# Down-projection weights of an expert loaded as two 64-partition transfers with two neighbouring rows per partition

## The chip, the cores and the metric

The kernel runs on one core of a Trainium2 chip. The metric is the device time of one execution in microseconds. Three runs of the kernel before gave 993.53, 995.6 and 988.67 us (median 993.53).

## The reference, cut to what matters

One step of a one-layer encoder over 320 tokens (256 of a prompt, 64 of a sample) of width 1024. Its first part (projections, mLSTM, spatial gating, memory attention, output projection) isn't touched. Its second part is a mixture of 32 experts of inner width 256, of which each token takes two out of one group of eight:

```
for e in range(N_EXPERTS):                                  # 32
    hidden = jax.nn.silu(xf @ w_g[e]) * (xf @ w_u[e])       # w_g, w_u: 1024 x 256
    y = y + combine[:, e:e + 1] * (hidden @ w_d[e])         # w_d: 256 x 1024
```

Each expert has three matrices of 1 MB in float32, so the mixture reads 96 MB of weights.

## The kernel before, in words

The program is written by hand, engine by engine, with semaphores. After the first part (until about 660 us of the span) comes `level`, the mixture. Up to 128 tokens of each of the four groups are gathered once, and then the 32 experts are taken in order, x = 0 to 31.

**Units of weights.** The list `STREAM` cuts the weights into 96 units of 1 MB: for each expert "A" (the first half of the rows of gate and up), "B" (the second half) and "D" (down). The order is A0 B0 A1 B1 D0 A2 B2 D1 and so on. There are six slots (`NS`), and unit u goes to slot u % 6. A slot holds the raw float32 unit (`raw_w`, 2048 numbers on each of 128 partitions), and beside it the same unit split into a high part and a rest (`w_r`), since a product is made of three products of such parts.

**Path of a unit.** SP (`load_unit`, L478) waits until PE has used the unit six places before (`m_used`), then issues two transfers of 512 KB, with 16 DMA engines below them (L498 for D, L503 for A and B). ACT waits for both (`m_full`) and copies the raw unit to its high part (`unit_high`, L889). DVE subtracts to get the rest (`unit_rest`, L1183). Then PE uses it: `gate_up` (L776) for A and B, `down` (L798) for D. The slot is free only when PE is done.

**Order on PE.** `gate_up` x part A, `hidden_T` of x - 1, `gate_up` x part B, `down` of x - 1, and on most experts a small `scatter` (L812) of the group before. `gate_up` is 12 matmuls of 512 columns for each part, `down` is 12. `hidden_T` (L786) transposes the hidden values of the expert (128 slots x 256, on DVE written to `hid` by L1481) with two transposes of 128 x 128 each, so that `hidT[:, .., c, :]` has on partition d the hidden index that the weights of `w_r[.., c*D : (c+1)*D]` have on partition d.

**Layout of D before.** The transfer k (0 or 1) puts rows k*128 to k*128+127 of the 256 x 1024 matrix on the 128 partitions, one row of 4 KB each. So partition d holds rows d and 128 + d, and transpose c takes the columns c*128 to c*128+127 of `hid`.

A and B have runs of 4 KB too: four rows of 256 numbers, on all 128 partitions.

Of the kernel before, what the change touches and what calls it, by code (L numbers as in the profile page):

```python
# [23 lines left out]
D = 1024  # L24
# [19 lines left out]
NS = 6  # L44
# [157 lines left out]
def build_kernel(nc, ins, outs):  # L202
    I, O = ins, outs
    ctx = ExitStack()
    with ctx:
# [109 lines left out]
        hid = at(SP0 + 3 * UW + G * 384, 2, DE)  # L315
# [26 lines left out]
        ident = sb("ident", [128, 128])  # L342
# [42 lines left out]
        ms = ctx.enter_context(nc.psum_tensor("ms", [128, 4, 512], FP32))  # L385
# [37 lines left out]
        m_full = [sem(f"expert_unit_full{i}") for i in range(NS)]  # L423
# [33 lines left out]
        @block.sync  # L457
        def _(sp):
            for i, (t0, n) in enumerate(TILES):
                src = I["x_prompt"][0, t0:t0 + n, :] if i < 2 else I["x_sample"][0, :, :]  # L460
                sp.dma_start(x_tm[0:n, i, :], src).then_inc(s_x, 16)
            for i in range(2):
                sp.dma_start(mem_tm[:, i, :], I["mem_prompt"][0, i * 128:(i + 1) * 128, :]).then_inc(s_mem, 16)
            for r0, name in ((P_MIX, "norm_mix_g"), (P_MEM, "mem_norm_g"), (P_MOE, "norm_moe_g"), (P_HN, "mlstm_norm_g")):
                sp.dma_start(prows[r0:r0 + 8, :], I[name][0, :].rearrange("(c p) -> c p", p=128)).then_inc(s_par2, 16)
            sp.dma_start(prows[P_CW:P_CW + 64, :], I["mlstm_conv_w"][0].rearrange("j (c p) -> (j c) p", p=128)).then_inc(s_par2, 16)
            sp.dma_start(prows[P_CB:P_CB + 16, :], I["mlstm_conv_b"][0, :].rearrange("(c p) -> c p", p=128)).then_inc(s_par2, 16)
            sp.dma_start(srows[0:48, :], I["state_mlstm_conv"][0, 0].rearrange("j (c p) -> (j c) p", p=128)).then_inc(s_par2, 16)
            sp.dma_start(srows[48:56, :], I["state_mlstm_n"][0, 0].rearrange("h (c p) -> (h c) p", p=128)).then_inc(s_par2, 16)
            for n, (name, col) in enumerate(UNITS):  # L470
                if n >= RING:
                    for e in "DP":
                        sp.wait_ge(u_lo[e], n - RING + 1)
                src = I[name][0, :, col:col + 256].rearrange("(k p) n -> p k n", p=128)
                sp.dma_start(ringw[:, n % RING, :].rearrange("p (k n) -> p k n", n=256), src).then_inc(unit_full[n % RING], 16)


            def load_unit(lv, u):  # L478
                x, part = STREAM[u]
                if isinstance(lv, int) and u < NS:  # L480
                    if u == 0:
                        sp.wait_ge(*done("gate", 1, 7))
                    elif u == 1:
                        sp.wait_ge(*done("br", 0, 7))
                    elif u == 2:
                        sp.wait_ge(*done("br", 1, 7))
                        sp.wait_ge(s_gvout, 16)
                    elif u == 4:
                        for e in "DP":
                            sp.wait_ge(u_lo[e], len(UNITS))  # L490
                else:
                    sp.wait_ge(m_used, NU * lv + u - NS + 1)
                if u == NS - 1:
                    sp.wait_ge(m_gather, NQ * (lv + 1))
                dst = raw_w[u % NS]
                if part == "D":
                    for k in range(2):
                        sp.dma_start(dst[:, k * D:(k + 1) * D], I["w_exp_down"][0, x, k * 128:(k + 1) * 128, :]).then_inc(m_full[u % NS], 16)  # L498
                else:
                    k0 = 0 if part == "A" else 4  # L500
                    for j, name in enumerate(("w_exp_gate", "w_exp_up")):
                        src = I[name][0, x].rearrange("(p k) n -> p k n", k=KC)[:, k0:k0 + 4, :]
                        sp.dma_start(dst[:, j * D:(j + 1) * D].rearrange("p (k n) -> p k n", n=DE), src).then_inc(m_full[u % NS], 16)  # L503

            for u in range(NU):
                load_unit(0, u)
            sp.wait_ge(*done("ranks"))
            need = sp.value_load(more[0:1, 0:1], min_val=0, max_val=LEVELS - 1)
            with sp.Fori(1, LEVELS) as lv:
                with sp.If(need >= lv):  # L510
                    for u in range(NU):
                        load_unit(lv, u)
            for i, (t0, n) in enumerate(TILES):
                sp.wait_ge(s_fin, i + 1)
                dst = O["y_prompt"][0, t0:t0 + n, :] if i < 2 else O["y_sample"][0]
                sp.dma_start(dst, y_tm[0:n, i, :]).then_inc(s_yout, 16)
            sp.wait_ge(s_yout, 48)
# [3 lines left out]
        def _(pe):  # L521
            mm, tr = nc.tensor.matmul, nc.tensor.transpose
# [12 lines left out]
            for s in STEPS:  # L535
# [7 lines left out]
                if s["ring"] == "pj":  # L543
                    n = s["unit"]
# [3 lines left out]
                if kind in ("mq", "qk", "o", "u", "gate", "br"):  # L548
                    c = a[-1]
                    src = xn_r  # L550
                    if kind == "mq":
                        pe.wait_ge(s_xnl, 3)
                    if kind == "br":
                        src = u_r if a[0] == 1 else br_r
# [6 lines left out]
                    last = project_parts(s, 128, T, lambda k, p, q: (w[:, p, k, (c % 2) * 128:(c % 2) * 128 + 128], src[:, q, k, :]))  # L561
                elif kind in ("memk", "memv"):
                    if kind == "memk":
                        pe.wait_ge(s_mnl, 2)
                    last = project_parts(s, 128, 256, lambda k, p, q: (mn_r[:, p, k, a[1] * 128:a[1] * 128 + 128], w[:, q, k, :]))
                elif kind in ("v", "gv"):
                    t0, n = TILES[a[1]]
                    last = project_parts(s, n, 256, lambda k, p, q: (xn_r[:, p, k, t0:t0 + n], w[:, q, k, :]))
                elif kind == "res":
                    t0, n = TILES[a[1]]  # L570
                    pe.wait_ge(s_mixl, 8)
                    last = project_parts(s, n, 256, lambda k, p, q: (mix_r[:, p, k, t0:t0 + n], w[:, q, k, :]))
                elif kind == "xT":
                    i, half = a
                    n = TILES[i][1]
                    pe.wait_ge(s_xs, i + 1)
                    for j in range(4):
                        last = tr(b[:, j * 128:j * 128 + n], xs_tm[0:n, i, (4 * half + j) * 128:(4 * half + j + 1) * 128], ident[0:n, 0:n])
                elif kind == "memT":
                    i, half = a  # L580
                    pe.wait_ge(s_xs, 4 + i)
                    for j in range(4):
                        last = tr(b[:, j * 128:j * 128 + 128], mem_tm[:, i, (4 * half + j) * 128:(4 * half + j + 1) * 128], ident[:, :])
                elif kind == "params":
                    pe.wait_ge(s_const, 2)
                    pe.wait_ge(s_par2, 16 * 8)
                    last = tr(b[:, 0:P_ALL], prows[0:P_ALL, :], ident[0:P_ALL, 0:P_ALL])
                elif kind == "state":
                    last = tr(b[:, 0:56], srows[0:56, :], ident[0:56, 0:56])
                elif kind in ("gi", "gf"):  # L590
# [3 lines left out]
                    last = project(s, H, T, [(wif[:, k, o:o + H], xnT[:, k, :]) for k in range(KC)])  # L594
                elif kind == "cols":
                    pe.wait_ge(s_g4, 1)
                    for i, (t0, n) in enumerate(TILES):
                        for q, r in enumerate((R_A, R_IG, R_F)):
                            c0 = (i * 3 + q) * H
                            last = tr(b[0:n, c0:c0 + H], rows[0:H, r, t0:t0 + n], ident[0:H, 0:H])  # L600
                elif kind == "bc":
                    last = mm(b[:, 0:T + TS + 1], sel[0:H, a[0], :], rb[0:H, :], start=True, stop=True)
                elif kind == "wsT":
                    pe.wait_ge(s_ws, 16)
                    for g in range(H):
                        last = tr(b[:, g * 128:g * 128 + 128], ws[:, g, :], ident[:, :])
                elif kind == "ka":
# [5 lines left out]
                    for dk in range(2):  # L613
                        for j in range(2):
                            src = memk[:, j, h * HD + dk * 128:h * HD + dk * 128 + 128] if which == 0 else cmk[:, h % 2, j, dk * 128:dk * 128 + 128]
                            last = tr(b[:, dk * 256 + j * 128:dk * 256 + j * 128 + 128], src, ident[:, :])
                elif kind == "sc":
# [3 lines left out]
                    for q, i in enumerate((0, 1) if which == 0 else (2,)):  # L621
                        t0, n = TILES[i]
                        for dk in range(2):
                            last = mm(b[0:n, q * 256:q * 256 + 256], mqT[:, 2 * h + dk, t0:t0 + n], kmT[:, h % 2, which, dk, :], start=dk == 0, stop=dk == 1)
                elif kind == "pt":
                    h, which = a
                    pe.wait_ge(s_prob, 2 * h + which + 1)
                    for j in range(2):
                        for i in ((0, 1) if which == 0 else (2,)):
                            n = TILES[i][1]  # L630
                            c0 = j * 256 + i * 128 if which == 0 else j * 64
                            last = tr(b[:, c0:c0 + n], probs[0:n, h % 2, i, j * 128:j * 128 + 128], ident[0:n, 0:n])
                elif kind == "av":
# [5 lines left out]
                    t0, n = (0, TP) if which == 0 else (TP, TS)  # L639
                    for dk in range(2):  # L640
                        for j in range(2):
                            v = memv[:, j, h * HD + dk * 128:h * HD + dk * 128 + 128] if which == 0 else cmv[:, h % 2, j, dk * 128:dk * 128 + 128]
                            last = mm(b[:, dk * n:dk * n + n], v, pT[:, h % 2, j, t0:t0 + n], start=j == 0, stop=j == 1)
                elif kind == "cvT":
                    pe.wait_ge(s_tail, 32)
                    last = tr(b[0:48, 0:128], cvo[:, a[0], :], ident[:, :])
                elif kind == "kt":
                    h, which = a
                    pe.wait_ge(s_silu, 8 + 2 * h + 2)
                    for i in ((0, 1) if which == 0 else (2,)):  # L650
                        t0, n = TILES[i]
                        for dk in range(2):
                            c0 = (i % 2) * 256 + dk * 128
                            last = tr(b[0:n, c0:c0 + 128], qkT[:, 8 + 2 * h + dk, t0:t0 + n], ident[:, :])
# [5 lines left out]
                elif kind == "num":  # L660
# [5 lines left out]
                    if i == 0:  # L666
                        last = mm(b[:, 0:w1], st[:, 0:128], v_tm[:, 0, h, 0:w1], start=True, stop=True)
# [112 lines left out]
            def hidden_T(lv, x):  # L780
                pe.wait_ge(m_hid, E * lv + x + 1)
                until(pe, m_htl, E * lv + x - 1)
                if x < 2:
                    pe.wait_ge(m_combined, lv + 1)
                for c in range(2):
                    last = tr(ms[:, x % 2, c * 128:c * 128 + 128], hid[:, x % 2, c * 128:c * 128 + 128], ident[:, :])  # L786
                last.then_inc(m_ht, 1)

            def down(lv, x):
# [895 lines left out]
```

## Time and profile before

| | us |
|---|---|
| median of three runs | 993.53 |
| the profiled execution | 991.24 |
| its span | 989.5 |
| PE busy in the span | 898.8 |
| DVE busy | 594.8 |
| ACT busy | 473.1 |

The span counts from the first instruction to the last, and 1.74 us of the profiled time lie around it. PE is the matmul engine, PEld its weight loads, which run beside it. DMA share is the mean busy share of the 16 DMA engines, GB/s is what they moved, and PEclk is the granted TensorE clock (1.00 is 2.4 GHz, 0.50 is 1.2 GHz).

### The profile page before, as it was taken

What the parts mean: (1) busy time and instruction counts of PE and PEld (TensorE: products, weight loads), DVE (VectorE), ACT (ScalarE), POOL (GpSimd) and SP (SyncE); (2) the same over time, 40 slices, a digit from 0 to 9 for tenths busy, and PEclk for the clock granted to TensorE, in tenths of its full rate; (3) what the DMA queues carried; (4) which work ended last, traced back from release to release, by engine and by line L of the source; (5) the groups of instructions that cost most, each with busy time, mean ns of one, the idle gap of its engine ahead of it and who ended that gap; (6) DMA issues with size and microseconds to landing.
All of it is one profiled execution on the core that took longest, in us unless ns stands there. A gap on an engine that the chain in (4) does not pass through costs nothing.

```text
span 989.5 us, 13338 instructions
## 1 busy us (share of the span) xinstructions
PE 898.8 (91%) x5322; PEld 796.4 (80%) x5322; DVE 594.8 (60%) x794; ACT 473.1 (48%) x571; POOL 250.9 (25%) x161
## 2 busy tenths in 40 slices
PE   1889999888999989888999999869999999999993
PEld 0588998878989889888999999838877887787881
DVE  2734257884133254378354444584888889889874
ACT  4344345442433133334323333357777677767752
POOL 3145543333442444243443444100000000000000
PEclk9999999998999999989999999969999999999996
DMA  8225642333347856943423348204999999999951
GB/s 244 85 91 166 213 154 81 97 97 116 123 148 97 108 157 88 138 139 119 148 88 126 128 128 276 108 0 174 350 353 348 352 347 343 350 348 355 348 201 56
DMA packets 102502, 182.68 MB, mean 185 GB/s; under 512 B 8345, under 2 KB 74593, under 8 KB 102434
## 3 DMA queue, kind: packets, MB, share of 16 engines
q1 hardware_dynamic: 95488, 171.55, 54.2%
q0 software_dynamic: 2640, 7.66, 3.6%
q10 hardware_dynamic: 4306, 2.54, 1.3%
q8 instruction: 45, 0.74, 0.3%
q14 instruction: 23, 0.19, 0.1%
HBM read 175.90 MB, written 5.82 MB: 184 GB/s over the span
## 4 chain that ended last, share of the span: by engine, by line
PE 55%; DMA 10%; DVE 5%; ACT 4%; POOL 2%; issue 2%; DVEq 0%; SPq 0%; ACTq 0%
PE pj L526 25%; PE pj L776 14%; PE pj L798 8%; DMA arena<-in_w_in 8%; POOL unit_r L1586 2%; DMA arena<-in_w_exp_down 2%; ACT unit_r L882 2%; PE ms L812 1%; PE ms L700 1%; PE ms L699 1%; ACT w_r L889 1%; DMA arena<-in_w_exp_up 1%; PE ms L526 1%; PE ms L741 1%; DVE w_r L1183 1%
## 5 line engine op out<-in xcount | busy, mean ns | idle before, releaser
L1586 POOL TENSOR_TENSOR unit_r<-arena,unit_r 128x1024 fp32r<-128x1024 f32 x64 | 210.4, 3289 | 326.9 <-ACT unit_r L882 326.9
L526 PE MATMUL pj<-xn_r,unit_r 128*128 128x320 f32 x1536 | 237.3, 313 | 9.6 <-POOL unit_r L1586 9.0
L1183 DVE TENSOR_TENSOR w_r<-arena,w_r 128x2048 fp32r<-128x2048 f32 x96 | 218.9, 2289 | 44.5 <-ACT w_r L889 44.2
L526 PEld LDWEIGHTS pj<-xn_r,unit_r 128*128 128x128 f32 x1536 | 228.4, 190 | 14.1 <-issue 12.7
L1174 DVE TENSOR_TENSOR unit_r<-arena,unit_r 128x1024 fp32r<-128x1024 f32 x64 | 85.0, 1329 | 233.5 <-ACT unit_r L882 233.5
L889 ACT ACTIVATE w_r<-arena 128x2048 fp32r<-128x2048 f32 x96 | 183.5, 1917 | 46.1 <-DMA arena<-in_w_exp_up 30.7
L776 PE MATMUL pj<-w_r,xg 128*128 128x512 f32 x768 | 190.8, 398 | 0.0
L776 PEld LDWEIGHTS pj<-w_r,xg 128*128 128x128 f32 x768 | 141.9, 189 | 30.5
L882 ACT ACTIVATE unit_r<-arena 128x2048 fp32r<-128x2048 f32 x64 | 121.9, 1905 | 62.2 <-PE pj L526 28.9
L798 PE MATMUL pj<-w_r,hidT 128*128 128x512 f32 x384 | 93.1, 391 | 3.0 <-DVE w_r L1183 1.5
L798 PEld LDWEIGHTS pj<-w_r,hidT 128*128 128x128 f32 x384 | 71.6, 188 | 20.1 <-DVE w_r L1183 3.6
L526 PE MATMUL pj<-unit_r,xn_r 128*128 128x256 f32 (+1 forms) x576 | 71.9, 286 | 6.3 <-POOL unit_r L1586 6.3
L526 PEld LDWEIGHTS pj<-unit_r,xn_r 128*128 128x128 f32 (+1 forms) x576 | 70.0, 177 | 6.8 <-issue 6.7
L526 PE MATMUL pj<-br_r,unit_r 128*128 128x320 f32 x384 | 59.7, 311 | 0.0
L526 PEld LDWEIGHTS pj<-br_r,unit_r 128*128 128x128 f32 x384 | 56.6, 188 | 1.4 <-issue 1.1
L526 PEld LDWEIGHTS pj<-unit_r,mn_r 128*128 128x128 f32 x384 | 48.0, 197 | 5.8 <-issue 4.7
L526 PE MATMUL pj<-unit_r,mn_r 128*128 128x256 f32 x384 | 49.6, 290 | 2.9 <-POOL unit_r L1586 2.9
L526 PE MATMUL pj<-unit_r,mix_r 128*128 128x256 f32 (+1 forms) x288 | 35.8, 288 | 2.2 <-DVE mix_r L1178 2.2
L526 PEld LDWEIGHTS pj<-unit_r,mix_r 128*128 128x128 f32 (+1 forms) x288 | 35.5, 178 | 2.5 <-issue 2.5
L1284 DVE SCALAR_TENSOR_TENSOR arena<-arena,prT 128x323 f32<-128x323 f32 x48 | 34.7, 722 | 1.7
L987 ACT ACTIVATE arena<-pj 128x320 f32<-128x320 f32 x24 | 10.4, 435 | 46.5 <-PE pj L526 46.4
L1074 ACT ACTIVATE hidT<-ms 128x256 fp32r<-128x256 f32 x32 | 12.3, 384 | 37.1 <-PE ms L786 36.7
(303 smaller groups left out, 844.9 us busy)
## 6 DMA issues: line engine op xcount, KB each, us to landing
arena<-in_w_in SPq DMA_DIRECT2D x40, 1024.0 KB, 5.3
arena<-in_w_exp_gate SPq DMA_DIRECT2D x64, 512.0 KB, 4.5
arena<-in_w_exp_up SPq DMA_DIRECT2D x64, 512.0 KB, 6.0
arena<-in_w_exp_down SPq DMA_DIRECT2D x64, 512.0 KB, 5.2
arena<-in_w_mem_k SPq DMA_DIRECT2D x4, 1024.0 KB, 11.3
arena<-in_w_mem_v SPq DMA_DIRECT2D x4, 1024.0 KB, 6.3
arena<-in_w_br_mem SPq DMA_DIRECT2D x4, 1024.0 KB, 7.7
arena<-in_w_br_mlstm SPq DMA_DIRECT2D x4, 1024.0 KB, 5.0
```

The lines of the kernel that those rows point to most:

```text
L526: last = mm(bank_of(s)[0:out_rows, 0:out_cols], l, r, start=k == 0, stop=k == len(pairs) - 1)
L699: mm(b[:, t0:t0 + n], gv_tm[0:n, i, c * 128:c * 128 + 128], wsT[0:n, g, 0:n], start=True, stop=False)
L776: last = mm(pj[:, x % 2, :].rearrange("p (h n) -> p h n", h=2), xg[:, k0 + k, xp, g * SLOTS:(g + 1) * SLOTS], w[:, wp, k, :, :], start=k0 ...
L798: last = mm(pj[:, 2 + half, :], hidT[:, x % 2, xp, c, :], w_r[u % NS][:, wp, c * D + half * 512:c * D + half * 512 + 512], start=e == 0 an ...
L882: af(unit_r[n % RING][:, 0, :], ringw[:, n % RING, :], ACT.Copy).then_inc(u_hi, 1)
L889: af(w_r[u % NS][:, 0, :], raw_w[u % NS], ACT.Copy).then_inc(m_hi, 1)
L987: af(sg[:, k % 2, :], b[:, 0:T], ACT.Sigmoid).then_inc(free, 1)
L1074: af(hidT[:, x % 2, 0, :, :].rearrange("p a b -> p (a b)"), ms[:, x % 2, 0:DE], ACT.Copy).then_inc(m_hth, 1)
L1174: v.tensor_tensor(unit_r[n % RING][:, 1, 0:UW // 2], ringw[:, n % RING, 0:UW // 2], unit_r[n % RING][:, 0, 0:UW // 2], ALU.subtract).then_ ...
L1183: v.tensor_tensor(w_r[u % NS][:, 1, :], raw_w[u % NS], w_r[u % NS][:, 0, :], ALU.subtract).then_inc(m_lo, 1)
L1284: ins = v.scalar_tensor_tensor(o, r[:, j:j + CONVW], w(j), o, ALU.mult, ALU.add)
L1586: g.tensor_tensor(unit_r[n % RING][:, 1, UW // 2:], ringw[:, n % RING, UW // 2:], unit_r[n % RING][:, 0, UW // 2:], ALU.subtract).then_inc ...
```

## The change

Both edits keep the count of instructions and their order on each engine. The two transfers of a D unit now have 64 partitions each: transfer q loads rows q*128 to q*128+127, with rows 2p and 2p+1 of that half side by side on partition q*64 + p, which is one run of 8 KB both in memory and on the partition. A partition d then holds rows 2d and 2d + 1 of the matrix. To match this, transpose c of the hidden values takes the columns 2d + c, every second one.

```
                 if part == "D":
-                    for k in range(2):
-                        sp.dma_start(dst[:, k * D:(k + 1) * D], I["w_exp_down"][0, x, k * 128:(k + 1) * 128, :]).then_inc(m_full[u % NS], 16)
+                    for q in range(2):
+                        src = I["w_exp_down"][0, x, q * 128:(q + 1) * 128, :].rearrange("(p c) n -> p (c n)", c=2)
+                        sp.dma_start(dst[q * 64:(q + 1) * 64, :], src).then_inc(m_full[u % NS], 16)
...
                 for c in range(2):
-                    last = tr(ms[:, x % 2, c * 128:c * 128 + 128], hid[:, x % 2, c * 128:c * 128 + 128], ident[:, :])
+                    last = tr(ms[:, x % 2, c * 128:c * 128 + 128], hid[:, x % 2, :].rearrange("p (d c) -> p c d", c=2)[:, c, :], ident[:, :])
```

All line numbers behind L498 grow by one in the changed kernel. A D unit is still 1 MB in two transfers of 512 KB, and the matmuls, their operands' sizes and the copies of ACT and DVE stay as they were.

## Rows read from the trace of the kernel before

**Rows 1.** The page, part 2: span in 40 slices (24.7 us each)

```profile
PE   1889999888999989888999999869999999999993
...
DMA  8225642333347856943423348204999999999951
GB/s 244 85 91 166 213 154 81 97 97 116 123 148 97 108 157 88 138 139 119 148 88 126 128 128 276 108 0 174 350 353 348 352 347 343 350 348 355 348 201 56
```

**Rows 2.** Busy time by stretch, mixture stage, and the last stretch one expert

```profile
core 0: us, PE busy (x) PEld busy (x) DVE busy (x) ACT busy (x) POOL busy (x), PEclk, DMA share, GB/s
700.00:750.00 50.00, 49.42 (x224) 39.52 (x223) 42.32 (x29) 36.88 (x31) 0.00 (x0) 1.00 0.98 349
850.00:900.00 50.00, 49.65 (x222) 40.27 (x221) 44.46 (x33) 35.05 (x28) 0.00 (x0) 1.00 0.99 349
900.00:950.00 50.00, 49.59 (x222) 40.14 (x221) 45.56 (x35) 35.71 (x32) 0.00 (x0) 1.00 0.98 348
680.00:968.00 288.00, 283.69 (x1260) 228.36 (x1259) 245.23 (x181) 197.88 (x166) 0.00 (x0) 1.00 0.93 330
891.38:900.36 8.98, 8.98 (x42) 7.33 (x41) 8.01 (x7) 5.92 (x4) 0.00 (x0) 1.00 1.00 352
```

**Rows 3.** Who waited for whom, 690 to 980 us: us, times, longest

```profile
DVE w_r L1183 <- ACT w_r L889: 33.2, 51, 1.6
ACT w_r L889 <- DMA arena<-in_w_exp_up: 28.7, 35, 2.2
ACT w_r L889 <- DMA arena<-in_w_exp_down: 15.0, 24, 1.2
```

**Rows 4.** The down transfers, all of them, from issue to landing

```profile
DMA to landing us min/median/max: 3.6/5.2/7.1
```

**Rows 5.** The store of y at the end: issues, then busy time by stretch

```profile
983.73 1.53 SPq L516 DMA_DIRECT2D out_y_prompt<-arena  x2
986.11 0.55 SPq L516 DMA_DIRECT2D out_y_sample<-arena  x1
...
985.00:987.00 2.00, 0.00 (x0) 0.00 (x0) 1.09 (x1) 0.00 (x0) 0.00 (x0) 0.50 1.00 406
987.00:988.00 1.00, 0.00 (x0) 0.00 (x0) 0.00 (x0) 0.00 (x0) 0.00 (x0) 0.50 0.89 217
988.00:989.00 1.00, 0.00 (x0) 0.00 (x0) 0.00 (x0) 0.00 (x0) 0.00 (x0) 0.50 0.45 98
```

**Rows 6.** The loads of x at the start: issues, then busy time by stretch

```profile
1.73 0.58 SPq L461 DMA_DIRECT2D arena<-in_x_sample  x1
2.35 1.06 SPq L463 DMA_DIRECT2D arena<-in_mem_prompt  x2
...
6.00:7.00 1.00, 0.00 (x0) 0.00 (x0) 0.00 (x0) 0.00 (x0) 1.00 (x3) 1.00 1.00 168
7.00:8.00 1.00, 0.00 (x0) 0.00 (x0) 0.00 (x0) 0.00 (x0) 0.50 (x1) 1.00 1.01 225
8.00:9.00 1.00, 0.00 (x0) 0.00 (x0) 0.00 (x0) 0.37 (x1) 0.00 (x0) 1.00 0.97 360
```

**Rows 7.** Instructions by line: the transposes, and two strided reads by ACT and DVE

```profile
L786 PEld LDWEIGHTS ms<-ident,arena x64: 137/140/144, 687.4 to 964.3; 128*128 128x128 f32 x64
L786 PE MATMUL ms<-ident,arena x64: 270/272/330, 687.7 to 964.4; 128*128 128x128 f32 x64
L893 ACT ACTIVATE hn_r<-arena x3: 2046/2057/2076, 643.2 to 647.9; 128x1024 fp32r<-128x1024 f32 x2, 64x1024 fp32r<-64x1024 f32 x1
L889 ACT ACTIVATE w_r<-arena x96: 1902/1919/1927, 615.9 to 958.8; 128x2048 fp32r<-128x2048 f32 x96
```

**Rows 8.** Busy time by stretch where the granted clock fell (columns of rows 2)

```profile
221.00:224.00 3.00, 0.00 (x0) 0.00 (x0) 2.89 (x6) 0.05 (x1) 2.31 (x5) 0.92 0.09 10
224.00:228.00 4.00, 2.38 (x6) 1.96 (x7) 3.82 (x9) 2.36 (x3) 0.61 (x1) 0.50 0.79 255
448.00:452.00 4.00, 1.27 (x10) 1.04 (x9) 3.83 (x7) 3.73 (x4) 3.52 (x2) 1.00 0.00 0
452.00:456.00 4.00, 4.00 (x19) 4.00 (x18) 3.96 (x2) 0.00 (x0) 2.19 (x1) 0.57 0.85 263
650.00:655.00 5.00, 5.00 (x14) 1.71 (x12) 5.00 (x3) 4.83 (x3) 0.00 (x0) 0.64 0.00 0
```

## The prediction

> **What bounds the kernel now.** I read the span in slices first [rows 1]. The change lies in the mixture, and the slices show that stage at once: from slice 29 to 38 both PE and the DMA engines stand at 9 tenths, at about 350 GB/s. Elsewhere the DMA engines are half idle, so the mixture is the one long stage in which a slower or faster transfer can count. Second, the busy time by stretch [rows 2]: in 50 us PE is busy for 49.4 to 49.7, and the DMA share is 0.98 or 0.99. For one expert, 891.38 to 900.36 us, PE is busy for 8.98 of 8.98 us. The DMA engines need for the same expert 3 x 1.049 MB = 3.146 MB / 0.350 MB per us = 8.99 us. So two resources are full at once, and neither has room. Over the whole stage, 680 to 968 us, PE lacks 288.0 - 283.7 = 4.3 us. Third, the waits [rows 3]: ACT waits 35 times for an "up" transfer and 24 times for a "down" transfer, 43.7 us in all, and DVE waits 51 times for ACT. The DMA already ends last at ACT, though the copies of ACT and DVE still hide it from PE. Fourth, issue to landing of the down transfers [rows 4]: 5.2 us in the middle for 512 KB, which at 350 GB/s take 1.5 us. So there is always work queued ahead of a transfer, and a slower transfer pushes back all that follow.
>
> **Part 1: transfers of 64 partitions.** What is new is not the bytes but the half of the partitions that each transfer writes. The trace has two transfers of 64 partitions and 4 KB runs, both in 256 KB, each next to transfers of 128 partitions. The store of y [rows 5]: the two prompt transfers move 406 GB/s at a share of 1.00. The sample transfer, with 64 partitions, follows: 217 GB/s at 0.89 (its first part still with the prompt in it), then 98 GB/s at 0.45, which is 98 / 0.45 = 218 GB/s with the engines busy. That is 0.54 of the full rate: all 16 engines are busy, each at about half speed. It is a store, so it reads SBUF where ours writes. The load of x_sample [rows 6] is a load, as ours: behind it the rate is 168 and 225 GB/s for 2 us at a share of 1.00, and 360 once it is through (the transfers behind it have 128 partitions, and share this stretch).
>
> The two halves of a D unit sit behind each other in the same queue, so I expect each engine to do its part of q = 0 and then of q = 1, and at any time most engines write to the same half. The price of a D unit is then 1.049 MB / 0.218 = 4.81 us in place of 1.049 / 0.350 = 3.00 us: 1.81 us more. I take this value, since it is from the row with the clearest cut between full and half width. The bounds: below, 0 us if loads don't show it or if the engines are so far out of step that they use both halves; even less than 0 if the 8 KB runs help (part 2). Above, from the load [rows 6]: (350 - 168) + (350 - 225) = 307 KB were lost in 2 us, which is 0.88 us at 350 GB/s, on a transfer of 0.262 MB; times four for a D unit, 3.5 us.
>
> The Trainium skill speaks against this change. "SBUF — State Buffer", section "Door 1: The DMA port swizzle", says that partitions 0 to 63 reach only half of the 16 ports, and that such a transfer of 1 MiB ran at 196 GB/s against 328 for all partitions. Its section "Can I just issue two DMAs to hit both halves?" says no: two transfers on the two halves were 6% faster than one. By it a D unit takes 1.049 / 0.208 = 5.04 us, 2.04 more than now, and the sum below would be 991.2 + 31 x 2.04 - 7 = 1047 us (an estimate from that page). The store in this trace agrees with it (218 GB/s at full share).
>
> How many D units count: D0 is in the first five units, which land before the stage (share 0.00 in 650 to 655 us, last of [rows 8]). That leaves 31 x 1.81 = 56.1 us of DMA time. What hides some of it: the DMA engines are idle for 1.6% of the 250 us from 700 to 950 us [rows 2], 4 us. And the load starts with a lead of the first units, of which about one unit (3 us) isn't used up now, as PE seldom waits. I take 56 - 4 - 3 = 49 us. Nothing else covers it: PE will wait for a D unit or for the A behind it, about 1.6 us per expert, with ACT and DVE waiting ahead of it. SP's next issue waits for PE in turn, and six slots don't help against a mean rate.
>
> **Part 2: runs of 8 KB.** There are half as many runs. No row shows 8 KB runs in a weight stream. As a bound for the gain, all of D at the clean 406 GB/s of [rows 5] would take 2.58 us, 0.42 less than 3.00: 13 us of DMA time over 31 units. Of these PE could win at most the 4.3 us that it lacks. The other bound is no gain, and I take 0, because the half width sets the rate.
>
> The skill's "DMA: Bandwidth & Descriptors", section "Why small descriptors are slow (HBM only)", gives a fixed cost of some 3 cycles per packet. For 4 KB (128 beats) that is 2.3%, and 8 KB would halve it: an estimate of 0.035 us for a D unit, 1 us in all. No run here shows it.
>
> **Part 3: strided transposes.** Two per expert, 64 in all, now read the hidden values with a step of 8 bytes. PE takes 272 ns for one, its weight load 140 ns [rows 7]. No row shows PE with a strided operand. Below: no change. Above: ACT reads 1024 numbers with a stride in 2057 ns (L893), where 2048 contiguous ones take 1919 ns (L889), so twice per number; twice for PE would be 0.27 us more for each, 64 x 0.27 = 17 us if nothing hid it. I take 0, because where PE waits 1.6 us per expert for the DMA, even the added 0.54 us per expert is covered. Without that cover (the first rival) up to 17 us would show.
>
> **Sum.** 991.2 (the profiled execution) + 49 + 0 + 0 = 1040 us. The profiled execution is 2.3 us under the median of the runs and inside their spread of 988.7 to 995.6, so I leave it so.
>
> **The rivals.**
>
> *A. Half width costs nothing in this stream, and the long runs pay.* For it: the two halves are issued within 1 us of each other, and 16 engines with separate backlogs could drift apart by more than the 1.3 us which a half takes at full rate, so that half the engines write low and half write high partitions. Against it: the drift would have to hold for all engines, as a unit is complete only with the slowest of them, and in [rows 6] the queue was as deep. Time: 991.2 - 4.3 = 987 us at best, 991 without a gain, up to 1008 with the transposes exposed. This is the case that ends on the other side; it decides from the point where a D unit takes under about 3.1 us.
>
> *B. Partly out of step.* The stalls of single engines put some pairs out of step, and half of the 1.81 us stays: 31 x 0.9 - 7 = 21 us, 1012 us.
>
> *C. The damage spreads as in the load at the start.* Engines with 128-partition work wait behind ports that are filled by others. 31 x 3.5 = 108.5, less 7: 102 us, 1093 us. For it is that [rows 6] is a load from the same kind of memory; against it, that other queues and cold buffers share those 2 us.
>
> *D. PE's clock falls in the new waits.* The clock was 0.50 or near it after PE had been busy for 0.00 of 3 us, and again after 1.27 of 4 us [rows 8]. At half clock an expert would need about 18 us of PE. But in my forecast PE is busy for 8.98 of 10.6 us and in one piece stands for under 2 us, so I give this 0.03; it would end above 1080 us.
>
> **How the numbers follow.** The forecast (1020 to 1065 us) has 0.62. B and its neighbours (1004 to 1020) 0.10. C and D (above 1065) 0.14. A has 0.14, of which 0.02 ends over 1% faster and 0.10 within 1%. A measurement of this kernel can tell about 1%, 10 us, from no change, so same is 984 to 1003 us. Slower: 0.62 + 0.10 + 0.14 + the 0.02 of A that is left = 0.88; I shade this to 0.86, same 0.11, faster 0.03. The range runs from 1006, under B, to 1078, between the forecast and C.
>
> **What would show it.** Right: in the changed profile the GB/s of the mixture slices fall from 350 to 290 to 310, with the DMA share still at 0.98 or more; PE falls to 8 tenths; the stretches in which a D unit is moved alone show 200 to 250 GB/s; ACT's wait for "down" grows from 15 us to far over 40; issue to landing of down grows from 5.2 us; L786 stays near 272 ns. Wrong: GB/s still near 350 with PE at 9 tenths (A); a DMA share well under 0.95 with PE waiting would mean that the issue or a wait, not the width, sets the pace; L786 at 400 ns or more would mean part 3 was priced wrongly; a granted clock under 1.00 in the stage is D.

## The result and the profile after

The changed kernel takes 1085.45 us (median of 4 runs, 1080.28 to 1088.63) against 991.43 us for the kernel before (4 runs, 988.67 to 995.6). The ratio is 1.094, with a 95% interval of 1.088 to 1.100: slower, as forecast, but by 94 us in place of 49, and outside my range of 1006 to 1078 us. The profiled execution took 1088.63 us, its span 1086.9 us. One execution of the experiment with sixteen units in a row and one of the looser wait fell in a slower state of the chip, and the ratios leave them out.

The page of the changed kernel, part 2 (40 slices of 27.2 us), which answers to [rows 1]:

```profile
PE   0989999989998997999999977987888877887783
DMA  7244642234558485443334710899999999899871
GB/s 222 78 149 145 212 136 87 89 97 130 131 104 124 99 152 100 154 127 116 117 124 148 271 39 16 248 289 244 244 262 247 267 261 254 243 279 256 222 188 51
```

Outside the mixture the rows have hardly changed. In it the DMA engines are about as busy as before, but move mostly 240 to 290 GB/s in place of 350, and PE falls from 9 tenths to 7 or 8. The stage fills about 13 slices of 27.2 us where it filled 11 of 24.7 us.

The busy time by stretch of the changed kernel (span times, busy time of each engine, granted clock, DMA share, GB/s), which answers to [rows 2] and has its columns:

```profile
700.00:950.00 250.00, 204.05 (x803) 159.09 (x802) 160.40 (x115) 132.08 (x109) 0.00 (x0) 0.92 0.97 256
```

An expert has 3.146 MB, so it now takes 3.146 / 0.256 = 12.3 us. At a share of 0.97 the DMA engines work for 11.9 us of it. Before, it was 9.0 us and 8.8. The stage is about 3 us per expert longer in work alone, where I had expected 1.8.

Who waited for whom in the mixture of the changed kernel (us in all, times, longest), which answers to [rows 3]:

```profile
DVE w_r L1184 <- ACT w_r L890: 129.4, 66, 3.8
PEld ms L787 <- DVE arena L1482: 77.1, 29, 4.1
ACT w_r L890 <- DMA arena<-in_w_exp_up: 75.4, 47, 4.1
ACT w_r L890 <- DMA arena<-in_w_exp_down: 69.0, 30, 3.1
```

Two things are to be seen. PE, which hardly waited, now waits for DVE's hidden values, and DVE in its turn was held by ACT and by the DMA. And ACT waits longer not only for "down", the transfer that was changed (15.0 before, 69.0 now), but just as much for "up", that is for the units A and B (28.7 before, 75.4 now), which were not touched. That was not in my working, and it points to where the missing time is. The page's part 6 says the same of issue to landing (KB each, us in the middle). Before, down took 5.2 us, and gate and up:

```profile
arena<-in_w_exp_gate SPq DMA_DIRECT2D x64, 512.0 KB, 4.5
arena<-in_w_exp_up SPq DMA_DIRECT2D x64, 512.0 KB, 6.0
```

In the changed kernel:

```profile
arena<-in_w_exp_gate SPq DMA_DIRECT2D x64, 512.0 KB, 6.5
arena<-in_w_exp_up SPq DMA_DIRECT2D x64, 512.0 KB, 11.3
arena<-in_w_exp_down SPq DMA_DIRECT2D x64, 512.0 KB, 8.4
```

The two transfers of a unit A or B are issued 0.4 us apart, one behind the other. The middle times of gate and up were 1.5 us apart before and are 4.8 us apart now. This is not the time of up by itself: the two transfers raise the same semaphore `m_full`, by 16 single steps each, and the profile gives the first 16 steps of a unit to gate and the last 16 to up, whichever transfer they came from. What has grown is the time between the first steps of a unit and its last one.

### The profile page after: what moved, and what is told of

Read it like the earlier page. It is cut to its first block, busy times and chain, and to the rows that moved or that the text cites. A ratio compares the mean times of both kernels' runs of the same rounds, so it can differ in the third digit from the quotient of the medians.

```text
span 1086.9 us, 13338 instructions
## 1 busy us (share of the span) xinstructions
PE 934.7 (86%) x5322; PEld 819.1 (75%) x5322; DVE 596.7 (55%) x794; ACT 474.4 (44%) x571; POOL 249.9 (23%) x161
## 4 chain that ended last, share of the span: by engine, by line
PE 39%; DMA 23%; DVE 5%; ACT 5%; issue 4%; POOL 2%; SPq 1%; DVEq 0%; ACTq 0%
PE pj L527 22%; DMA arena<-in_w_exp_down 17%; DMA arena<-in_w_in 7%; PE pj L777 6%; PE pj L799 4%; ACT w_r L890 3%; POOL unit_r L1587 2%; ACT unit_r L883 1%; PE ms L701 1%; PE ms L787 1%; PE ms L700 1%; PE ms L742 1%; DVE arena L1500 1%; SPq L499 1%; PE pj L742 1%
## 5 line engine op out<-in xcount | busy, mean ns | idle before, releaser
L527 PE MATMUL pj<-xn_r,unit_r 128*128 128x320 f32 x1536 | 240.3, 316 | 9.4 <-POOL unit_r L1587 9.2
L527 PEld LDWEIGHTS pj<-xn_r,unit_r 128*128 128x128 f32 x1536 | 231.3, 192 | 14.1 <-issue 12.2
L777 PE MATMUL pj<-w_r,xg 128*128 128x512 f32 x768 | 217.4, 438 | 0.0
L777 PEld LDWEIGHTS pj<-w_r,xg 128*128 128x128 f32 x768 | 161.4, 214 | 37.0
L787 PE MATMUL ms<-ident,arena 128*128 128x128 f32 x64 | 17.2, 354 | 64.5 <-DVE arena L1482 64.5
L787 PEld LDWEIGHTS ms<-ident,arena 128*128 128x128 f32 x64 | 10.3, 206 | 77.4 <-DVE arena L1482 77.1
```

The costliest lines, as they stand in the source:

```text
L527: last = mm(bank_of(s)[0:out_rows, 0:out_cols], l, r, start=k == 0, stop=k == len(pairs) - 1)
L777: last = mm(pj[:, x % 2, :].rearrange("p (h n) -> p h n", h=2), xg[:, k0 + k, xp, g * SLOTS:(g + 1) * SLOTS], w[:, wp, k, :, :], start=k0 ...
```

## The experiments

All ratios are to the kernel before on the same chip; these chips ran it at 982 to 991 us, so ratios are compared and not times. Two theories were at odds at first. *Width*: the 64 partitions of a transfer make the damage. *Layout*: the 8 KB runs or the strided transposes do.

**One part at a time.** First the layout alone, as an edit of the changed kernel: 128 partitions, 4 KB runs, rows 2d and 2d + 1 on partition d, strided transposes.

```
-                    for q in range(2):
-                        src = I["w_exp_down"][0, x, q * 128:(q + 1) * 128, :].rearrange("(p c) n -> p (c n)", c=2)
-                        sp.dma_start(dst[q * 64:(q + 1) * 64, :], src).then_inc(m_full[u % NS], 16)
+                    for c in range(2):
+                        src = I["w_exp_down"][0, x].rearrange("(p c) n -> p c n", c=2)[:, c, :]
+                        sp.dma_start(dst[:, c * D:(c + 1) * D], src).then_inc(m_full[u % NS], 16)
```

> A D unit comes in two transfers of 128 partitions with 4 KB runs again, but rows 2d and 2d+1 still meet on partition d and the transposes still take every second column. Width theory (the 64 partitions make the damage): 991 us plus what the strided transposes cost on a PE that is full; their weight load grew from 140 to 198 ns in the changed kernel, so 64 x 0.06 to 0.1 us = 4 to 7 us, 995 to 998 us. Rival (the strided transposes, or the new order of rows in memory, make it): 1050 us or more.

Measured: ratio 1.002 (0.9993 to 1.0046).

Second, again from the changed kernel, 8 KB runs on 128 partitions, in one transfer (the counts that ACT waits for follow the number of transfers, here and below; those lines are left out):

```
-                    for q in range(2):
-                        src = I["w_exp_down"][0, x, q * 128:(q + 1) * 128, :].rearrange("(p c) n -> p (c n)", c=2)
-                        sp.dma_start(dst[q * 64:(q + 1) * 64, :], src).then_inc(m_full[u % NS], 16)
+                    src = I["w_exp_down"][0, x].rearrange("(p c) n -> p (c n)", c=2)
+                    sp.dma_start(dst, src).then_inc(m_full[u % NS], 16)
```

> One transfer of 1 MB on 128 partitions with 8 KB runs for a D unit, transposes strided. Width theory: as with 4 KB runs on 128 partitions, 990 to 998 us, mixture at about 350 GB/s. Rival (8 KB runs are slow by themselves, or one large packet blocks others): 1040 us or more.

Measured: ratio 0.998 (0.9961 to 1.0006).

Third, the width alone, as an edit of the kernel before: 64 partitions, with 4 KB runs and the contiguous transposes of before.

```
-                    for k in range(2):
-                        sp.dma_start(dst[:, k * D:(k + 1) * D], I["w_exp_down"][0, x, k * 128:(k + 1) * 128, :]).then_inc(m_full[u % NS], 16)
+                    for q in range(2):
+                        src = I["w_exp_down"][0, x].rearrange("(k p) n -> p k n", k=2)[q * 64:(q + 1) * 64, :, :]
+                        sp.dma_start(dst[q * 64:(q + 1) * 64, :].rearrange("p (k n) -> p k n", k=2), src).then_inc(m_full[u % NS], 16)
```

> Two transfers of 64 partitions, but with the layout of before: two runs of 4 KB on each partition, transposes contiguous. Width theory: the whole damage is here, 1078 to 1090 us, about 255 GB/s. Rival (run length or strided transposes): under 1010 us. A part of each: in between.

Measured: ratio 1.092 (1.0885 to 1.095), the whole of the damage. So layout falls: the long runs and the strided transposes together do nothing that these runs can tell, and the width does everything. The transposes did become dearer on PE, in the changed kernel and in the strided run alike. The rows of the strided run (minimum, median, maximum in ns), against [rows 7]:

```profile
L787 PEld LDWEIGHTS ms<-ident,arena x64: 194/198/223, 673.7 to 956.5; 128*128 128x128 f32 x64
L787 PE MATMUL ms<-ident,arena x64: 270/282/388, 673.9 to 956.6; 128*128 128x128 f32 x64
```

198 ns for the weight load in place of 140, 64 x 0.058 = 3.7 us if all of it showed; the interval allows between -1 and +5 us.

**Width, or half of the partitions?** A pair with the same sizes, counts and 8 KB runs, three transfers for a D unit each. The control keeps each transfer in one half; the other lays the large one across the middle. The lines that differ:

```
-                    for p0, p1 in ((0, 64), (64, 96), (96, 128)):
+                    for p0, p1 in ((32, 96), (0, 32), (96, 128)):
                         src = I["w_exp_down"][0, x, 2 * p0:2 * p1, :].rearrange("(p c) n -> p (c n)", c=2)
                         sp.dma_start(dst[p0:p1, :], src).then_inc(m_full[u % NS], 16)
```

> Control for the next run. A D unit in three transfers with 8 KB runs: partitions 0-63, then 64-95, then 96-127. Each transfer stays in one half (0-63 or 64-127). Theory (it counts which half of the partitions is written at a time, not how many partitions): as the changed kernel, ratio 1.08 to 1.11 to before. Rival (the count of 64 partitions in a transfer is what matters): the 32-partition transfers would be worse, over 1.12.

> The same three sizes, but the 64-partition transfer lies across the middle, partitions 32-95, so that it writes both halves; then 0-31 and 96-127. Theory of halves: one half of a D unit runs at full width again, so half the dose; by the run with every second expert, half the dose costs about a quarter of the damage: ratio 1.02 to 1.05. Rival (64 partitions are slow wherever they lie): the same as the control within 1%.

Measured: 1.089 (1.0807 to 1.0969) for the control and 1.026 (1.0189 to 1.0332) across the middle. Busy time by stretch, control:

```profile
700.00:950.00 250.00, 202.25 (x820) 158.00 (x818) 163.07 (x116) 134.13 (x111) 0.00 (x0) 0.94 0.98 264
```

and across:

```profile
700.00:950.00 250.00, 226.83 (x973) 179.00 (x972) 194.56 (x142) 160.47 (x133) 0.00 (x0) 0.99 0.99 312
```

The trace also has the duration of each DMA packet. In these two runs a packet of 8 KB belongs to a D unit and one of 4 KB to A or B. From 700 to 950 us the D packets of the control take 609 ns on average, and those of the run across the middle 472 ns, where half of the bytes are in the transfer with both halves (8 KB packets on 128 partitions take 351 ns in the run with long runs). So a transfer of 64 partitions isn't slow by itself. It is slow where all 64 lie in one half. This agrees with the Trainium skill, "SBUF — State Buffer", section "Door 1: The DMA port swizzle", whose table gives partitions 0 to 63 the even ports and 64 to 127 the odd ones, so that 32 to 95 reach all 16.

**Is the dose linear?** Sixteen half-width D units, the others with 128 partitions in the same layout (the transfers of the strided run): once at every second expert, once in a row for experts 0 to 15. One line differs between the two:

```
-                    if x % 2:
+                    if x < 16:
```

> The changed kernel for odd experts, transfers of 128 partitions with the same layout for even ones. If each half-width unit has its own price (94 us / 31 units = 3 us), half of it: 991 + 48 = 1039 us. If the damage comes mostly from engines that get out of step and stay so, it grows with the number of half-width units in a row, or the queue between them absorbs some: 1010 to 1030 us.

> Sixteen half-width units as in the run with every second expert, but in a row: experts 0 to 15 by the changed kernel, 16 to 31 by transfers of 128 partitions with the same layout. Theory (half-width units one after another put the engines out of step, which adds about 1.2 us per expert to the 1.8 us of the unit itself; full-width units between them bring the engines together again): 15 x 3.0 = 45 us less a few us, ratio 1.035 to 1.048, with the first half of the mixture at about 257 GB/s and the second at about 345. Rival (each half-width unit costs the same, and the full dose has another reason, such as a share that only shows when all of the stage is slow): the same as every second expert, ratio 1.016 to 1.029.

Measured: 1.022 (1.016 to 1.0289) for every second expert, 1.040 (1.0331 to 1.0473) for the same number in a row. So the price of a half-width unit depends on what its neighbours are: 0.022 x 982 = 22 us for 16 of them apart, 1.4 us each; 0.040 x 991 = 40 us for 16 in a row, of which the first is loaded ahead of the stage, 2.6 us each. In the changed kernel it is 94 / 31 = 3.0 us each. The 22 us are what the sum of my forecast gives for 16 units, 16 x 1.81 - 7 = 22; the dose in a row is where it fails. With every second expert the middle times of gate and up are also close again, 5.5 and 6.6 us.

**Engines in step.** My theory by now: a unit is complete only when the slowest of 16 engines has done its share. While some engines are still at D in one half, others are at A or B, whose data goes to both halves, and would meet them there; so what D costs is laid on A and B too. If so, a wait that holds the engines together must lower the DMA work, though it adds idle time. First the tight wait:

```
                 if part == "D":
+                    if isinstance(lv, int):
+                        sp.wait_ge(*loaded(lv, u - 1))
                     for q in range(2):
```

> The changed kernel, with one wait on SP: a D unit is issued only when the unit ahead of it has landed on all engines. It brings the 16 engines into step before every half-width unit and empties the queue. Theory (part of the damage is that engines out of step write half-width data beside the full-width data of others): the GB/s while D is moved stay near 218, but A and B return to about 350 GB/s; each expert then takes 2 x 3.0 + 4.8 + about 2 us for the empty queue = 12.8 us, against 12.2 in the changed kernel: ratio 1.09 to 1.13, but with the median issue to landing of gate and up 1.5 to 2 us apart in place of 4.8. Rival (A and B are slow for another reason): A and B stay slow and the 2 us come on top, 14 us per expert, ratio 1.15.

Measured: 1.126 (1.1183 to 1.1329), 3.146 / 0.240 = 13.1 us per expert. The long row is 700 to 950 us; the others are one expert of this run, with D issued at 858.58 us and the next D at 871.14 us:

```profile
700.00:950.00 250.00, 194.90 (x749) 151.98 (x749) 150.72 (x109) 123.41 (x104) 0.00 (x0) 0.89 0.82 240
...
861.00:863.00 2.00, 2.00 (x11) 1.64 (x10) 1.71 (x3) 0.66 (x1) 0.00 (x0) 1.00 1.11 254
863.00:865.00 2.00, 2.00 (x11) 1.65 (x10) 0.98 (x1) 0.00 (x0) 0.00 (x0) 1.00 0.97 197
865.00:867.00 2.00, 2.00 (x10) 1.65 (x9) 0.00 (x0) 0.82 (x1) 0.00 (x0) 1.00 0.97 309
867.00:869.00 2.00, 1.19 (x6) 0.61 (x4) 0.87 (x1) 1.79 (x3) 0.00 (x0) 1.00 1.05 420
869.00:871.00 2.00, 0.00 (x0) 0.00 (x0) 2.00 (x3) 1.48 (x1) 0.00 (x0) 1.00 0.70 279
```

A packet is counted whole in the stretch in which it starts, so a short stretch can show a share above 1. Here one can watch a half-width unit nearly by itself: about 225 GB/s for the 4 us from 861 to 865 us with all engines busy, then up to 420 GB/s once A and B are moved, then the idle that the wait makes. (The kernel before has single stretches of 2 us at up to 412 GB/s too, so 420 is not out of the common.) The share is 0.82, so the engines work for 0.82 x 13.1 = 10.7 us per expert. That is 1.2 us less than the 11.9 us of the changed kernel, for the same bytes through the same halves. My forecast, in work, was 8.8 + 1.8 = 10.6 us. The middle times of gate and up are 7.7 and 8.5 us, 0.8 apart in place of 4.8.

Then a looser wait, on the unit two places ahead (u - 2):

> The changed kernel, with a looser wait on SP: a D unit is issued when the unit two places ahead has landed on all engines, so the queue holds one unit when D comes and doesn't run empty, and no engine can be more than a unit ahead. Theory of step: less time lost to engines out of step than in the changed kernel and less idle than with the tight wait: ratio 1.06 to 1.085. Rival (the order of the engines doesn't matter, only the sum of the transfers): 1.09 to 1.10.

Measured: 1.058 (1.0523 to 1.0629). Busy time by stretch:

```profile
700.00:950.00 250.00, 213.35 (x885) 168.68 (x884) 175.08 (x127) 144.85 (x121) 0.00 (x0) 0.95 0.98 284
```

A wait added to a DMA-bound stage made it faster than the changed kernel by 3.3% (1.058 against 1.094), slightly more than I had allowed. An expert takes 3.146 / 0.284 = 11.1 us with the engines at work for 10.9 us. This leaves 0.058 x 991 = 57 us, or 1.8 us for each of 31 units: about the price of the halves alone.

**Single packets and steps.** A shorter queue could also be what helps, without any engines in step. The traces can tell more. They have the size and duration of every packet and the time of every step of `m_full`. The table is for 700 to 950 us; work is the mean duration of a packet times the packets of a 1 MB unit, over 16 engines. "Both" is the share of time in which packets of D and of A or B are under way at once. "Apart" is the median time from the first to the last of the 32 steps of an A or B unit.

| run | work of a D unit, us | work of an A or B unit, us | both | apart, us |
|---|---|---|---|---|
| before (all packets 4 KB, no telling apart) | 2.93 | 2.93 | - | 3.3 |
| 8 KB runs on 128 partitions | 2.81 | 2.96 | 0.37 | 3.3 |
| changed kernel | 4.88 | 3.43 | 0.76 | 6.9 |
| every second expert | 4.73 (half width) | 2.82 (all 4 KB packets) | 0.13 | 2.6 |
| tight wait | 4.78 | 2.96 | 0.07 | 1.7 |
| looser wait | 4.79 | 3.02 | 0.27 | 3.1 |

The D unit costs nearly the same wherever it is half-width. What changes is A and B: 0.50 us more for each in the changed kernel, and nearly nothing more where the steps of a unit lie close together. Within the changed kernel the 4 KB packets take 178 ns where no D packet is under way, and 236 ns where one is; in the run with 8 KB runs on 128 partitions the pair is 183 and 190 ns. So packets of full-width units are slowed while half-width ones are under way, and in the changed kernel that is most of the time. A shorter queue isn't needed for it: with every second expert no wait was added, and the 4 KB packets are fast too. These records don't name the engine of a packet, so which engines fall behind, and why, stays open.

**The clock.** In the changed kernel the granted clock fell again and again (0.92 in the stage). An example, of the changed kernel:

```profile
771.00:773.00 2.00, 0.00 (x0) 0.00 (x0) 1.34 (x1) 0.90 (x2) 0.00 (x0) 1.00 1.07 236
773.00:775.10 2.10, 0.70 (x3) 0.70 (x4) 1.35 (x2) 1.16 (x1) 0.00 (x0) 0.86 0.97 172
775.10:778.90 3.80, 3.80 (x13) 2.95 (x12) 2.63 (x2) 1.73 (x3) 0.00 (x0) 0.63 0.85 251
```

PE was busy for 0.70 of the 4.1 us ahead of the last stretch, and there 12 matmuls of `gate_up` took 4.47 us, where 12 of them had taken 2.96 us at a clock of 1.00 shortly before. To see whether that counts, PE was given something to do in the wait:

```
+                until(pe, m_htl, E * lv + x - 1)
+                if x >= 2:
+                    for _ in range(8):
+                        mm(ms[:, x % 2, 0:512], xg[:, 0, 0, 0:128], xg[:, 0, 0, 0:512], start=True, stop=True)
                 pe.wait_ge(m_hid, E * lv + x + 1)
-                until(pe, m_htl, E * lv + x - 1)
```

> The changed kernel, with 8 matmuls of 512 columns (1.9 us) that nobody reads put on PE ahead of the wait for the hidden values in every expert from the third on, where PE waited up to 4.1 us in the changed kernel. If the fall of the granted clock (0.50 for 3.4 us in about every second expert) costs time on the loop of slots, the clock stays at 1.00 and the time falls by up to 1.4 us x 16 = 22 us, ratio 1.07. If the DMA engines alone set the pace, the clock stays up and the time stays within 1% of the changed kernel, ratio 1.085 to 1.10.

Measured: 1.090 (1.0821 to 1.0983). Busy time by stretch:

```profile
700.00:950.00 250.00, 230.86 (x1002) 184.43 (x1001) 167.78 (x120) 137.20 (x115) 0.00 (x0) 0.99 0.99 269
```

The clock stayed at 0.99, and the time is that of the changed kernel within the intervals (1.094). So the slower matmuls lie in time that PE has to spare behind the DMA engines.

**Is there something to win with the long runs?** Two more forms, both on 128 partitions. In the first, DVE writes the hidden values in the order of the transposes:

```
-                v.scalar_tensor_tensor(hid[:, x % 2, :], pj[:, x % 2, DE:2 * DE], comb[:, x:x + 1], sgh[:, x % 2, :], ALU.mult, ALU.mult)...
+                v.scalar_tensor_tensor(hid[:, x % 2, :].rearrange("p (c d) -> p d c", c=2), pj[:, x % 2, DE:2 * DE].rearrange("p (d c) -> p d c", c=2), comb[:, x:x + 1], sgh[:, x % 2, :].rearrange("p (d c) -> p d c", c=2), ALU.mult, ALU.mult)...
```

> A try at the best of both: one transfer of 1 MB on 128 partitions with 8 KB runs, and DVE writes the hidden values in the order that the transposes want, so that PE reads them contiguously again and DVE reads and writes with a stride. If the strided transposes cost the few tenths of a per cent between the two layouts, 0.993 to 1.000 of before; if DVE pays more for its strides (its product took 476 ns), 1.00 to 1.01.

Measured: 1.001 (0.999 to 1.0038). The stride moved to DVE, whose product takes 682 ns there in place of 477 (medians).

The other form is the layout of before, in one transfer of 1 MB:

```
-                    for k in range(2):
-                        sp.dma_start(dst[:, k * D:(k + 1) * D], I["w_exp_down"][0, x, k * 128:(k + 1) * 128, :]).then_inc(m_full[u % NS], 16)
+                    src = I["w_exp_down"][0, x].rearrange("(k p) n -> p k n", k=2)
+                    sp.dma_start(dst.rearrange("p (k n) -> p k n", k=2), src).then_inc(m_full[u % NS], 16)
```

> The layout of before (4 KB runs, two rows 128 apart on a partition, contiguous transposes), but a D unit in one transfer of 1 MB in place of two of 512 KB. It tells whether the run of long runs gained by the run length or by one issue less. Either way 0.994 to 1.002.

Measured: 1.003 (1.0003 to 1.0059), just above my range. The long runs are worth nothing that can be measured here, whichever engine takes the stride; no form beats the kernel before clearly.

## Why the prediction was right or wrong

**What bounds the kernel.** Right. PE and the DMA engines were both full, and a loss on the DMA side came through to the end.

**Part 1, the mechanism.** Right, and shown: a transfer into one half of the partitions is slower, at about 0.6 of the rate (2.93 / 4.88). The width alone gives 1.092 of 1.094, and a transfer of the same size across the middle loses much less.

**Part 1, the price of a unit.** 1.81 us, from the store at the end [rows 5], was nearly right: a D unit costs 4.88 - 2.93 = 1.95 us more, 0.14 x 31 = 4 us in all. With the waits, the work per expert is 10.7 and 10.9 us, against 10.6 forecast.

**Part 1, the count.** This is the step that failed: "31 x 1.81 = 56.1 us of DMA time", which takes each D unit for itself and leaves A and B at their old speed. In the changed kernel A and B cost 3.43 us of work each and not 2.93: 1.0 us per expert, 31 us of the 45 that were missing. It goes when a wait keeps the units from overlapping, and when full-width units lie between. I had written out this case as rival C ("the damage spreads as in the load at the start"), 1093 us, and it came within 8 us. Its mechanism fits what the packets show. That its number came so near is partly luck: its 3.5 us for a unit are more than the 1.95 + 1.0 us of work that were measured, and its credit of 7 us did not come. I had set [rows 6] aside as the fault of other queues, when they could as well be read as transfers of 128 partitions slowed beside a half-width one. And I had used being out of step only as a relief (rivals A and B), never as a cost.

**The credit.** I took off 4 us because idle time of the DMA engines would be filled. It wasn't: the share is 0.97 of 12.3 us, 0.37 us idle per expert where it was 0.02 x 9.0 = 0.18, so idle grew by 0.19 x 31 = 6 us, and with the credit this is 10 us of the 45. With the 31 and the 4 us above the sum is 45, closer than such rounded shares deserve. No run tests the 3 us taken off for the lead.

**Part 2, the long runs.** Taking 0 was right: 0.998 with 8 KB runs, 1.003 with one transfer of 4 KB runs.

**Part 3, the transposes.** I took 0 and bounded it by 17 us. The weight load grew by 58 ns, and exposed on a full PE the two strided transposes cost 0.2% (interval -0.1% to +0.5%), which can't be told from nothing. "L786 stays near 272 ns" was wrong as a sign: its middle (now L787) is 384 ns in the changed kernel. The stride is the small part of that: it is 282 ns in the strided run, and 282 ns too in the run that kept the clock at 0.99.

**Rival D, the clock.** It fell, to which I had given 0.03, but it cost nothing that shows: my price for it presumed a PE at half clock throughout, and in the changed kernel the clock was 0.92 over the stage, in time that PE had to spare.

## What to carry to other kernels

Keep transfers that carry a DMA-bound stage on all 128 partitions, or at least across both halves (32 to 95 does it); longer runs don't make up for half the width. Price a slow transfer in a queue by what it does to its neighbours too: look at the waits and the packets of transfers that were not changed. Where fast and slow transfers overlap because the 16 engines have drifted apart, a wait that brings them together may pay, even in a stage bound by DMA: here it won back 3.3% of the changed kernel, and stayed 5.8% behind the kernel before.

## What the runs showed of the hardware that was not expected

- The same 16 half-width units cost 22 us with full-width units between them and 40 us in a row. The first and the last step of an A or B unit lie 6.9 us apart in the changed kernel (median) and 2.6 us apart with every second expert.
- Packets of transfers that reach both halves are slowed by half-width ones under way beside them: 236 ns against 178 ns in the changed kernel.
- A wait on SP for an earlier unit took the ratio from 1.094 to 1.058, by raising 256 to 284 GB/s at nearly the same share (0.97 and 0.98).
- A float32 transpose with a step of two elements makes the weight load 198 ns in place of 140, where ACT took twice the time per number for its strided read [rows 7].
